# First attention by steps of two heads, with value products in plain fp32

## What is computed

```python
def chunked_attention(q, k, v, q_gain, k_gain, rel_bias):
    q = rmsnorm(q.reshape(B, S, N_HEADS, HEAD_DIM), q_gain)      # 8 heads of 64
    k = rmsnorm(k.reshape(B, S, N_HEADS, HEAD_DIM), k_gain)
    ...
        s = jnp.einsum('bqhd,bkhd->bhqk', qb, kb).astype(jnp.float32) * scale + bias
        s = jnp.where(valid[None, None], s, NEG_INF)
        p = jax.nn.softmax(s, axis=-1)
        return jnp.einsum('bhqk,bkhd->bqhd', p.astype(vb.dtype), vb)
```

## Time and profile before

| | us |
|---|---|
| median of 3 runs | 1620.23 |
| lowest, highest run | 1619.55, 1625.07 |
| profiled execution, its time | 1629.48 |
| its span, first to last instruction | 1627.7 |
| TensorE matmul busy in the span | 1584.7 (97%) |
| VectorE busy | 777.2 (48%) |
| ScalarE busy | 588.4 (36%) |
| POOL busy | 77.8 (5%) |
| mean granted TensorE clock | 0.985 of 2.4 GHz |

### The profile page before, as it was taken

The page is one execution under the profiler, slowest core; times in us unless marked ns, Lnnn a source line. Parts: engine busy times, 40 slices in busy tenths (PEclk is TensorE's granted clock), DMA queues, the critical chain, the costliest instruction groups (busy, mean ns, idle before and its releaser), DMA issues.

```text
span 1627.7 us, 19432 instructions
## 1 busy us (share of the span) xinstructions
PE 1584.7 (97%) x7222; PEld 1284.6 (79%) x7222; DVE 777.2 (48%) x1141; ACT 588.4 (36%) x976; POOL 77.8 (5%) x66
## 2 busy tenths in 40 slices
PE   7999999999999999999999999999999999999998
PEld 5888888878867788888888878777778788888886
DVE  3444422455355664444323465687554643234424
ACT  6222221234245533322212273445543434223322
POOL 0000000001012120000000051100000000000000
PEclk9999999999999999999999999999799999999999
DMA  5333343333211133333333333321123233233232
GB/s 171 94 99 94 91 104 96 98 104 110 78 49 40 43 104 93 101 91 103 91 103 91 103 95 99 105 79 39 40 80 102 78 91 103 91 93 100 91 104 91
DMA packets 246027, 147.67 MB, mean 91 GB/s; under 512 B 17472, under 2 KB 230096, under 8 KB 245840
## 3 DMA queue, kind: packets, MB, share of 16 engines
q1 hardware_dynamic: 232896, 141.58, 29.1%
q10 hardware_dynamic: 13072, 5.31, 1.3%
HBM read 142.66 MB, written 4.21 MB: 90 GB/s over the span
## 4 chain that ended last, share of the span: by engine, by line
PE 89%; DVE 5%; ACT 3%; issue 1%; DMA 1%; SPq 0%; POOL 0%; DVEq 0%; ACTq 0%; POOLq 0%
PE bank L352 29%; PE bank L356 28%; PE bank L355 28%; DVE w_low L1117 1%; ACT w_high L599 1%; PE bank L2073 1%; DMA w_raw<-in_ffn_w_up 1%; PE bank L2356 0%; PE bank L1980 0%; DVE d_s L1455 0%; DVE c_acc L1478 0%; PE bank L2061 0%; PE bank L2141 0%; DMA w_raw<-in_w_out 0%; PE bank L2237 0%
## 5 line engine op out<-in xcount | busy, mean ns | idle before, releaser
L352 PE MATMUL bank<-region,w_high 128*128 128x512 f32 (+1 forms) x1484 | 590.0, 398 | 9.8 <-DVE w_low L1117 4.0
L356 PE MATMUL bank<-region,w_low 128*128 128x512 f32 (+1 forms) x1484 | 581.6, 392 | 0.0
L355 PE MATMUL bank<-region,w_high 128*128 128x512 f32 (+1 forms) x1484 | 581.5, 392 | 0.0
L1117 DVE TENSOR_TENSOR w_low<-w_raw,w_high 128x1024 fp32r<-128x1024 f32 (+1 forms) x259 | 334.4, 1298 | 150.0 <-ACT w_high L599 146.4
L599 ACT CAST w_high<-w_raw 128x1024 fp32r<-128x1024 f32 (+1 forms) x259 | 265.6, 1028 | 261.9 <-DMA w_raw<-in_ffn_w_down 107.3
L352 PEld LDWEIGHTS bank<-region,w_high 128*128 128x128 f32 (+1 forms) x1484 | 280.3, 189 | 79.0 <-DVE w_low L1117 8.6
L356 PEld LDWEIGHTS bank<-region,w_low 128*128 128x128 f32 (+1 forms) x1484 | 280.3, 189 | 60.8
L355 PEld LDWEIGHTS bank<-region,w_high 128*128 128x128 f32 (+1 forms) x1484 | 280.6, 189 | 57.1
L352 PE MATMUL bank<-w_high,region 128*128 128x512 f32 x416 | 166.2, 400 | 4.7 <-DVE w_low L1117 1.7
L356 PE MATMUL bank<-w_high,region 128*128 128x512 f32 x416 | 163.4, 393 | 0.0
L355 PE MATMUL bank<-w_low,region 128*128 128x512 f32 x416 | 163.2, 392 | 0.0
(11 more groups left out here) (266 smaller groups left out, 1306.8 us busy)
## 6 DMA issues: line engine op xcount, KB each, us to landing
w_raw<-in_ffn_w_down SPq DMA_DIRECT2D x48, 512.0 KB, 3.9
w_raw<-in_ffn_w_gate SPq DMA_DIRECT2D x44, 512.0 KB, 3.7
w_raw<-in_ffn_w_up SPq DMA_DIRECT2D x44, 512.0 KB, 3.7
w_raw<-in_w_in SPq DMA_DIRECT2D x40, 512.0 KB, 3.8
w_raw<-in_w_up SPq DMA_DIRECT2D x32, 512.0 KB, 4.0
w_raw<-in_w_down SPq DMA_DIRECT2D x32, 512.0 KB, 3.5
w_raw<-in_w_out SPq DMA_DIRECT2D x16, 512.0 KB, 3.8
region_f<-in_x SPq DMA_DIRECT2D x4, 512.0 KB, 7.0
```

Source lines behind the costliest of these rows:

```text
L352: mm = pe.matmul(out, a_hi, b_hi, start=start, stop=False)
L355: pe.matmul(out, a_hi, b_lo, start=False, stop=False)
L356: return pe.matmul(out, a_lo, b_hi, start=False, stop=stop)
L1117: last = dve.tensor_tensor(piece(w_low[b % RING]), piece(w_raw[b % RING]), piece(w_high[b % RING]).bitcast(F32), ALU.subtract)
```

## The change

The loop goes by steps w = 0 to 17 instead of units: step w is a pair of heads p = w // 4 and a query block q = w % 4, so unit 2w is the even head and 2w + 1 the odd head. Scores of both heads are issued together, into banks 4 and 5; transposes of both into banks 6 and 7. The transposed probabilities are copied once, unsplit, by ScalarE for the even head and VectorE for the odd one, into `plain`, a view of fp32. The values are kept unsplit as well (VectorE alone writes them). The value products are plain fp32, one instruction for each head and key block, with 64 output rows each: rows 0 to 63 of bank p % 2 for the even head, 64 to 127 for the odd one. Four bias buffers take the place of two. One normalisation of 128 rows serves two heads. The spread's eight products alternate between the halves. The K-steps of u stand by a table, `fill`, of up to two at one place. The other side tasks (weight parts, pooled parts, u tiles, parts of the output) move to the steps that the diff shows.

```diff
-                bias = sb("bias", [P, 2, S], F32, s2)
+                bias = sb("bias", [P, 4, S], F32, s2)
...
+        plain = over[2][:, 8:13, :].rearrange("p a b -> p (a b)").rearrange("p (b n) -> p b n", n=P)
...
-            for i in range(TT):
-                act.wait_ge(acc_ready, RES["v"] + i + 1)
-                act.activation(part[2][:, i, :], bank[(RES["v"] + i) % BANKS][:], ACT.Identity,
-                               scale=r_col[:, i:i + 1]).then_inc(ev_hi, 1)
...
+            def a_turned_even(w):
+
+                p, q = divmod(w, TT)
+                act.wait_ge(a_turned, 2 * w + 1)
+                if p >= 1:
+                    act.wait_ge(a_weighed, 8 * (p - 1) + 2 * q + 1)
+                act.copy(plain_unit(0, q), bank[6][:, 0:(q + 1) * P].rearrange("p (k n) -> p k n", n=P)).then_inc(a_thi, 1)
...
+            for w in range(2 * HEADS + 2):
+                p, q = divmod(w, TT)
+                for c in range(2):
+                    if w < 2 * HEADS:
+                        a_expo(2 * w + c)
+                    if c == 0 and 1 <= w <= 2 * HEADS:
+                        a_turned_even(w - 1)
+                if w < 2:
+                    toeplitz(w + 2)
+                if q >= 2 and 2 * p + q < HEADS:
+                    bias_copy(2 * p + q)
+                    if 2 * p + q + 2 < HEADS:
+                        toeplitz(2 * p + q + 2)
+                if w >= 5 and q == 1:
+                    a_spread_copy(p - 1)
+                if w >= 10 and q == 2:
+                    a_pair_hi(p - 2)
+                if w in (5, 8, 12):
+                    pooled_hi((5, 8, 12).index(w))
+                if w in (1, 4, 8, 12):
+                    split_hi(BLK["u"] + (1, 4, 8, 12).index(w) + AHEAD)
+            pooled_hi(3)
+            a_pair_hi(2)
             a_pair_hi(3)
-            pooled_hi(3)
...
-            values_lo("v", 0, 3)
+            for i in range(TT):
+                acc = result(RES["v"] + i)
+                dve.tensor_scalar(over[2][:, i, :], acc[:], r_col[:, i:i + 1], None, ALU.mult).then_inc(acc_free, 1)
...
+                dve.tensor_tensor(a_full[:, p % 2, :], bank[p % 2][:], a_bc[:, p % 2, :], ALU.mult).then_inc(a_normed, 1)
...
+            for w in range(2 * HEADS + 2):
+                p, q = divmod(w, TT)
+                if w in (4, 9, 14):
+                    u_tile(w // 5 + 1, bank[3])
+                if w >= 5 and q == 1:
+                    a_invert(p - 1)
+                if w < 2 * HEADS:
+                    a_min_of(2 * w)
+                    a_min_of(2 * w + 1)
+                if 1 <= w <= 2 * HEADS:
+                    a_turned_odd(w - 1)
+                if w >= 9 and q == 1:
+                    a_norm(p - 2)
+                if w >= 10 and q == 2:
+                    a_pair_lo(p - 2)
+                if w in (5, 8, 12):
+                    pooled_lo((5, 8, 12).index(w))
+                if w in (1, 4, 8, 12):
+                    split_lo(BLK["u"] + (1, 4, 8, 12).index(w) + AHEAD)
+            a_norm(3)
+            pooled_lo(3)
+            a_pair_lo(2)
             a_pair_lo(3)
-            pooled_lo(3)
...
+            def a_scores(w):
+
+                p, q = divmod(w, TT)
+                n = (q + 1) * P
+                for c in range(2):
+                    if w >= 1:
+                        pe.wait_ge(a_biased, 2 * w + c - 1)
...
+                    rows_ = slice(64 * c, 64 * c + 64)
+                    split3(pe, bank[4 + c][:, 0:n], part[1][rows_, p, q * P:(q + 1) * P], part[1][rows_, 8 + p, q * P:(q + 1) * P],
+                           part[1][rows_, 4 + p, 0:n], part[1][rows_, 12 + p, 0:n], True, True).then_inc(a_score, 1)
+
+            def a_weigh(p, k):
+
+                if k == 0:
+                    pe.wait_ge(a_thi, 4 * p + 4)
+                    pe.wait_ge(a_tlo, 4 * p + 4)
+                    if p >= 2:
+                        pe.wait_ge(a_normed, p - 1)
+                for c in range(2):
+                    pe.matmul(bank[p % 2][64 * c:64 * (c + 1), k * P:], over[2][:, k, P * p + 64 * c:P * p + 64 * (c + 1)],
+                              plain_keys(c, k), start=k == 0, stop=k == TT - 1).then_inc(a_weighed, 1)
...
+            fill = (2, 2, 2, 2, 2, 2, 2, 1, 1, 2, 2, 1, 1, 2, 0, 0, 0, 0)
+            for w in range(2 * HEADS + 2):
+                p, q = divmod(w, TT)
+                if w < 2 * HEADS:
+                    a_scores(w)
+                if w >= 5:
+                    for k in range((w - 5) % TT, TT if w == 2 * HEADS + 1 else (w - 5) % TT + 1):
+                        a_weigh((w - 5) // TT, k)
+                if 1 <= w <= 2 * HEADS:
+                    a_turn(w - 1)
+                if q >= 2 and 2 * p + q < HEADS:
+                    a_bias(2 * p + q)
+                side_steps("u", DT + sum(fill[:w]), DT + sum(fill[:w + 1]), x_in1)
+                if w >= 5 and q == 1:
+                    a_spread_sums(p - 1)
```

More of the change, by code:

```diff
@@ L286, in build, with plain_unit, plain_keys @@
         turned = part[2][:, 8:18, :].rearrange("p a b -> p (a b)").rearrange("p (s b n) -> p s b n", s=2, n=P)
+        plain = over[2][:, 8:13, :].rearrange("p a b -> p (a b)").rearrange("p (b n) -> p b n", n=P)
+        def plain_unit(c, q):
+            first, step = (15 - 5 * q, 6) if c else (q + 1, 5)
+            return plain[:, first:first + step * q + 1:step, :]
+        def plain_keys(c, k):
+            first = 5 * (3 - k) if c else 6 * k + 1
+            return plain[:, first:first + TT - k, :].rearrange("p b n -> p (b n)")
         def turned_unit(h, q, low):
@@ L751, in _ @@
                 act.copy(part[1][:, i, :], qk_full[:, i % 2, :]).then_inc(qk_hi, 1)
[L752 to L755 removed]
             def bias_copy(h):
                 act.wait_ge(b_mm, h + 1)
[L760 to L763 removed]
+                if h >= 4:
+                    act.wait_ge(a_biased, 2 * TT * (h // 2 - 1))
+                act.copy(bias[0:64, h % 4, 256:448], bank[2][0:64, 0:192])
+                act.copy(bias[64:128, h % 4, 256:512], bank[2][64:128, 0:256]).then_inc(b_done, 1)
             act.wait_ge(qk_lo, 8)
@@ new lines, in a_turn @@
+            def a_turn(w):
+                q = w % TT
+                for c in range(2):
+                    u = 2 * w + c
+                    pe.wait_ge(a_exp, u + 1)
+                    if w >= 1:
+                        pe.wait_ge(a_tlo if c else a_thi, w)
+                    for k in range(q + 1):
+                        place = k if c == 0 else q - k
+                        mm = pe.transpose(bank[6 + c][:, place * P:(place + 1) * P], a_p[:, u % 3, k * P:(k + 1) * P], CI(C_IDENT))
+                    mm.then_inc(a_turned, 1)
@@ L2058, in a_spread_sums @@
                     pe.wait_ge(a_spread_out, p)
-                for q in range(2 * TT):
-                    r, c = 64 * (q // TT), q % TT * P
-                    mm = pe.matmul(bank[2][r:r + 64, c:c + P], a_rec[:, 8 * p + q:8 * p + q + 1].broadcast_to([P, 64]), CI(C_IDENT),
-                                   start=True, stop=True)
+                for q in range(TT):
+                    for c in range(2):
+                        at = 8 * p + TT * c + q
+                        mm = pe.matmul(bank[2][64 * c:64 * (c + 1), q * P:(q + 1) * P], a_rec[:, at:at + 1].broadcast_to([P, 64]),
+                                       CI(C_IDENT), start=True, stop=True)
                 mm.then_inc(a_spread, 1)
```

113 lines of the change are left out of this document (26 added, 87 removed).

## The result

| | us |
|---|---|
| before, median of 4 runs | 1619.95 (1619.55 to 1625.07) |
| after, median of 4 runs | 1604.95 (1603.56 to 1606.41) |
| ratio | 0.9887, 95% interval 0.9863 to 0.991 |
| after, profiled execution and its span | 1604.41, 1602.6 |
| mean granted TensorE clock in it | 0.989 |

The change makes the kernel 15.0 us faster; forecast were 14.7, and 1605.5 us.

What follows compares the result with a forecast made beforehand. The first attention lasts as long as TensorE's matmuls. Savings of 10.6, 5.3, 1.6 and 1.8 make 19.3 us; less waits of 0.5, 0.7 and 1.7 and clock 1.7, 14.7, so 1605.5 us, range 1600.5 to 1609.

Steps and rivals of the forecast that it cites:

- Scores, -10.6: First attention: two heads' score units run side by side, so 21.1 us becomes 10.6, saving 10.6.
- Value products, -5.3: First attention: plain fp32 products of two heads in both column halves take 10.5 us instead of 15.8, saving 5.3.
- Full overlap of column halves: Value products: two heads' products run fully side by side; without overlap 18.8 us instead of 10.5, 8.3 between the ends.
- Spread, -1.6: Spread of the inverse sums: with halves taking turns each takes 1.1 us instead of 1.51, four times, saving 1.6.
- u projection, -1.8: First attention: 24 single K-steps at 0.89 us, 21.4, become 10 places with two and 4 with one, 19.6.
- Transposes, 0: First attention: the 80 transposes are the same in number, so their time was taken as unchanged, 0.
- Waits, +2.9: First attention: new TensorE waits of 0.5 us at step 3, 0.7 at step 9 and 1.7 in the last steps.
- Clock, +1.7: Before the output projection: TensorE idles some 2.6 us, then 3.4 us run at granted clock 0.51, costing 1.7.
- the column halves don't run side by side: Rival, value products: no overlap, so 8.3 us come back and 7.4 are saved, 1612.8 us; chance 0.11.
- ScalarE and VectorE become the bound: Rival, first attention: 0.4 us more waiting in each of 16 steps, saved 8.3, 1611.9 us; chance 0.12.
- The scores don't pair: Rival, scores: the second unit waits for bank 5 at each step, saved only 4.1, 1616.1 us; chance 0.03.
- slower by the clock: Rival, first attention: holes in the stretch make the granted clock fall, 1615 to 1636 us; chance 0.03.

Runs made afterwards that it cites:

- e2: The changed kernel with a K-step, or where there is none the value products, between the two heads' scores of a step; 1622.4 us, stretch 78.7.
- e1: The changed kernel with the odd head's value products sent to output rows 0 to 63 too, added to the even head's; 1610.45 us, stretch 67.8.
- e3: The changed kernel with the spread in its old order, four products of one half, then four of the other; one run, 1614.4 us.
- e5: The changed kernel with the last spread and inversion ahead of the last value products, and the second pair's output parts moved from step 14 to 16; 1598.76 us.
- e6: The changed kernel with high and low parts kept and three value products of 128 output rows per head and block; 1614.34 us, stretch 72.6.
- e7: The kernel before, units in old order, with plain fp32 value products of 64 output rows and one ScalarE copy, no parts; 1627.1 us, stretch 85.4.
- e9: e7 with 128 output columns a value product, half of them used; one run, 1631.38 us, stretch 90.5.

## Why the prediction was right

The direction and the time (1605.5 against 1604.95) were right, and so was the main reason: the stretch is TensorE's, and the halves of its array work side by side.

- **Scores, -10.6:** measured -10.6 (21.8 to 11.2). With the waits in both taken off (0.52 and 0.47) it is 21.3 to 10.8, -10.5. e2 shows that it hangs on the heads standing side by side.
- **Value products, -5.3:** 17.4 to 11.9 is -5.5, but 1.36 of the 11.9 is a wait; the products themselves fell by 6.9. Those of after are as forecast, 10.5. The mis-sized part is before: I took 1.98 us a head from the earlier trace rows, where twelve products stand together, for all eight heads; the other seven have theirs in four places each, and the mean was 2.2.
- **Full overlap of column halves:** the open term, with 8.3 us between its ends. e1 measures 7.2 for the stretch.
- **Spread, -1.6:** -1.9. e3, which undoes it alone, gives 1.9 too.
- **u projection, -1.8:** this step failed. Measured -0.1, or -0.5 without the wait at step 3. The places after are as forecast (476.46 to 478.02, 1.56 us for two), but before the 24 K-steps took 19.6 us, 0.82 each, not 0.89: the price in the earlier trace rows is that of a K-step between two units of scores, and it was taken for all of them. The timeline of the kernel before shows what the others cost: 20 of the 24 have transposes, bias products or value products behind them, work of 128 rows with no change of shape, and take 0.79 to 0.82 us; the four that have scores or the spread behind them take 0.89 or 0.90. One of the 20, 0.80 us:

```profile
482.76 0.50 PE L352 MATMUL bank<-region,w_high 128*128 128x512 f32 x1
...
483.56 0.49 PE L2073 MATMUL bank<-const,a_p 128*128 128x128 f32 x3
```

- **Transposes, 0:** without their waits they fell by 1.0, from 11.3 to 10.3. This was a term that I had at nothing, and it makes up for most of the one above. The transposes of two heads now stand together, with fewer changes of shape; that this is the cause was not tried by itself.
- **Waits, +2.9:** 3.18 us idle against 0.98 before, 2.2 more. Step 9 0.53 (0.7 forecast), last steps 2.19 (1.7). Step 3 was forecast as 0.5 for the second head's scores; they start 0.47 late, as forecast, but the first head's wait as well, 0.37, so the step costs 0.84. The mechanism of the last one was only half seen: I laid the chain out from the end of the last scores with the reduction starting at once, and it started behind the output part, as e5 shows.
- **The way to the output projection, 5.3:** 5.27.
- **Clock, +1.7:** this did not come. Between the pooling and the output projection TensorE stood idle for 1.34 us, not for 2.6, since the pooling products were held back too and ended at 540.5, and the clock stayed at 1.00. The part of the sum that the clock took was paid all the same, but elsewhere: the executions of the change in the result had a lower mean clock than most of before's.

TensorE's work fell by 20.2 (19.3 forecast), waits and idle time took 2.2 (2.9), and the clock in the stretch nothing (1.7): -17.9 up to the output projection, where -16.4 was forecast and -14.7 with the clock's fall behind it. The median's 15.0 is this less some 3 us of clock, and to that extent its match with the forecast is luck. ScalarE and VectorE came down to 38.4 and 35.2 us, where 38 and 34 were forecast. Two of the prediction's sums are off by a little: 4 x 2.6 is 10.4, not 10.5, and 1620.2 less 19.3 is 1600.9, not 1600.5; nothing rests on either. What stays open is whether the change makes the lower clock likelier: its ten runs lie at 0.989 to 0.993, and 13 of the 45 of before above that, but e5, which differs from it in the last steps only, reached 0.994 and 0.995 in 3 of 5.

Of the rivals, "the column halves don't run side by side" was priced at 7.3 us less gain than the forecast, and e1 measures 7.2. "ScalarE and VectorE become the bound" did not happen, but e6 shows how near it is: with the parts kept TensorE is idle for 3.5 us more. "The scores don't pair" and "slower by the clock" came together in e2, in which the whole gain was gone. The Trainium skill ("TensorE: Matmul & The Clock Gate", Part 3) lets weight loads overlap with products only where the row group differs. The value products use all 128 rows in both halves and overlap fully, 1.01 us against 1.86 in e1, so here the measurement decides against the rule.

## What to carry to other kernels

Neither half of this change was worth the whole: plain values alone made the stretch 6.8 us longer, the order alone made it shorter by 8.6 to 9.4 of the 18.0 (its fall of the clock taken off), and only together did two products of 64 columns fill both halves of the array in the time of one. Put products for different halves directly behind one another, and count about 0.2 us for each excursion into another shape and back; a price for a small piece of work must be read at all the kinds of place where it stands, not at one. When the time and a stretch disagree by a few microseconds, set the runs against their granted clock before looking for a cause in the code.

## What the runs showed of the hardware

- Two products on different column halves, with different streams of 128 rows each, take the time of one: 1.01 us for two heads of 512 plain fp32 columns, 1.86 in the same half.
- Eight small products that alternate between column halves take 1.0 us, in blocks by halves 1.5, with the same instructions.
- An excursion into another shape and back costs about 0.2 us (4.7 us in 24 places, e7 against e9); a K-step behind scores takes 0.80 us with work of its own shape behind it and 0.90 with another shape there (24 K-steps of the kernel before).
- The granted clock fell from its upper to its lower level 0.5 us after TensorE had waited for 2.61 us (e2), 2.1 us after it had waited for 2.06 us, with 0.83 more up to the fall (e3), and 0.8 us after it had waited for 1.77 us, with 0.45 more around the fall (e6). It did not fall after 1.36 with 0.83 behind it, nor after 1.34 (the change). But it also fell at 475.9 and 476.0 in e9 and e2, where the idle time ahead was 0.93 us as in the kernels of before and after, in which it didn't; for that no cause is shown here.
